# First attention: the odd key tiles split into high and low parts as the even ones are, and the low parts made behind the row maxima

## What is computed

```python
s = (jnp.einsum('bqhd,bkhd->bhqk', qn_b, k_nope, preferred_element_type=jnp.float32)
     + jnp.einsum('bqhr,bkr->bhqk', qr_b, k_rope, preferred_element_type=jnp.float32))
p = jax.nn.softmax(s * scale, axis=-1).astype(v.dtype)
return jnp.einsum('bhqk,bkhd->bqhd', p, v)
```

## Time and profile before

| | |
|---|---|
| median of three runs | 3052.82 us |
| the profiled execution | 3052.03 us |
| its span from first to last instruction | 3050.3 us |
| granted TensorE clock, mean of the span | 0.991 of full speed |
| TensorE (matmul) busy | 2938.4 us, 96% |
| VectorE busy | 1974.5 us, 65% |
| ScalarE busy | 1462.9 us, 48% |

### The profile page before, as it was taken

How to read it: one execution, slowest core, us unless ns; L and a number is a source line. 1 busy time by engine, 2 the same in 40 slices (tenths; PEclk the granted TensorE clock), 3 DMA queues, 4 the chain that set the end, 5 groups by cost and what they waited for, 6 DMA issues and landing times. The chain is left out here.

```text
span 3050.3 us, 46806 instructions
## 1 busy us (share of the span) xinstructions
PE 2938.4 (96%) x18638; PEld 2340.8 (77%) x18638; DVE 1974.5 (65%) x3424; ACT 1462.9 (48%) x2678; POOL 0.2 (0%) x4
## 2 busy tenths in 40 slices
PE   8999999999999999999999989889899999999998
PEld 4676666688888888888888878777778887778886
DVE  4755766658666657877555476777655676656775
ACT  5324555645333334564334377566533555454443
POOL 0000000000000000000000000000000000000000
PEclk9999999999999999999999999999999999999999
DMA  7530000052333347553333342000054334456654
GB/s 277 198 127 1 1 1 1 15 166 73 90 104 104 104 136 272 179 176 104 111 111 110 124 131 58 30 24 24 3 171 167 125 104 145 148 189 241 239 187 148
DMA packets 257018, 359.75 MB, mean 118 GB/s; under 512 B 12832, under 2 KB 142496, under 8 KB 253600
## 3 DMA queue, kind: packets, MB, share of 16 engines
q1 hardware_dynamic: 256800, 356.76, 35.2%
HBM read 272.29 MB, written 84.41 MB: 117 GB/s over the span
## 5 line engine op out<-in xcount | busy, mean ns | idle before, releaser
L206 PE MATMUL ps<-ffn_h,wh 128*128 128x512 f32 x2176 | 671.7, 390 | 6.3 <-DVE ob L1372 5.4
L443 DVE TENSOR_TENSOR wl<-wr,wh 128x512 fp32r<-128x512 f32 x610 | 402.3, 686 | 300.0 <-ACT wh L419 297.6
L419 ACT ACTIVATE wh<-wr 128x512 fp32r<-128x512 f32 x610 | 360.4, 624 | 454.7 <-PE ps L206 345.1
L206 PEld LDWEIGHTS ps<-ffn_h,wh 128*128 128x128 f32 x2176 | 407.4, 188 | 95.3 <-DVE ob L1372 9.6
L206 PE MATMUL ps<-ffn_h,wl 128*128 128x512 f32 x1088 | 423.4, 389 | 0.0
L206 PE MATMUL ps<-in_h,wh 128*128 128x512 f32 x1200 | 369.9, 389 | 2.1 <-DVE ob L1372 2.1
L206 PE MATMUL ps<-wh,wh 128*128 128x512 f32 x756 | 294.8, 390 | 3.3 <-DVE wl L443 3.1
L206 PE MATMUL ps<-wh,wl 128*128 128x512 f32 x756 | 294.2, 389 | 0.0
L206 PE MATMUL ps<-wl,wh 128*128 128x512 f32 x756 | 294.1, 389 | 0.0
L206 PEld LDWEIGHTS ps<-in_h,wh 128*128 128x128 f32 x1200 | 225.0, 188 | 49.4 <-DVE ob L1372 2.5
L206 PEld LDWEIGHTS ps<-ffn_h,wl 128*128 128x128 f32 x1088 | 204.3, 188 | 42.5
(11 more groups left out here) (407 smaller groups left out, 5258.0 us busy)
## 6 DMA issues: line engine op xcount, KB each, us to landing
hid<-ob SPq DMA_DIRECT2D x174, 256.0 KB, 2.3
wr<-hid SPq DMA_DIRECT2D x84, 512.0 KB, 4.8
wr<-in_w_down SPq DMA_DIRECT2D x72, 512.0 KB, 4.3
wr<-in_w_up SPq DMA_DIRECT2D x54, 512.0 KB, 4.4
wr<-in_w_in SPq DMA_DIRECT2D x42, 512.0 KB, 4.8
kept<-ob SPq DMA_DIRECT2D x84, 256.0 KB, 2.0
late<-in_w_ada SPq DMA_DIRECT2D x16, 1024.0 KB, 5.9
wr<-in_w_out SPq DMA_DIRECT2D x32, 512.0 KB, 4.4
```

Source lines behind the costliest of these rows:

```text
L206: return e.op.matmul(out, left, right, start=start, stop=stop, skip_group_check=True)
L419: e.op.activation(self.rows(s)[0], src, ACT.Copy).then_inc(*e.event(self.name + "_act", ("w_high", self.name, s)))
L443: e.op.tensor_tensor(lo, src, hi.bitcast(F32), ALU.subtract).then_inc(*e.event(self.name + "_dve", ("w_low", self.name, s), *done))
```

## The change

1. Odd key tiles are split too: `exponential` makes `Ph` for every step, `low` makes `Pl` for every step, `value` is an `mm3` for every step. The values of the odd key tiles get a high and a low part `VOh`, `VOl` instead of `V1`; their side job gains one subtraction.
2. In `step_vector` the low part of step n + 1 moves from the front of the step to behind the side job and the maxima, for all n.
3. The split exponentials get four pairs of tiles, three of which lie in the first 12 KB, where `X` lies; `VOl` lies there as well. So the loads of `x` move to the queue of the output projection, and wait until the last `value` is done.

```diff
@@ __init__, parts
-        self.V1 = [k.sb("V1", [128, 5, 128], 34.5 + 32 * i) for i in range(2)]
+        self.VO = [pair("VO", [128, 5, 128], (34.5 + 32 * i, 16 + 2.5 * i)) for i in range(2)]
-        self.P = [pair("P", [128, 512], at) for at in ((178, 180), (37, 53), (128, 130))]
+        self.P = [pair("P", [128, 512], at) for at in ((178, 180), (0, 2), (4, 6), (8, 10))]
...
-        i = n // 2 % 2
-        return self.P[2 if i and n >= self.STEPS - 20 else i]
+        return self.P[n % 4]
@@ value
-        if n % 2 == 0:
-            e.wait_ge(("p_low", n))
-            x = mm3(e, o, [x[:, kt // 2, :] for x in self.V[h % 2]], [x[:, :] for x in self.parts(n)], kt == 0, False)
-        else:
-            e.wait_ge(("exp", n))
-            x = mm(e, o, self.V1[h % 2][:, kt // 2, :], self.E[n % 4][:, :], False, kt == 9)
+        e.wait_ge(("p_low", n))
+        V = (self.V, self.VO)[n % 2][h % 2]
+        x = mm3(e, o, [x[:, kt // 2, :] for x in V], [x[:, :] for x in self.parts(n)], kt == 0, kt == 9)
@@ exponential
-        e.wait_ge(("score", n), (("value" if n % 2 else "p_low"), n - 4) if n >= 4 else None)
+        e.wait_ge(("score", n), ("p_low", n - 4) if n >= 4 else None)
         e.op.activation(x, self.bank(n % 3), ACT.Exp).then_inc(*e.event("att_exp", ("exp", n)))
-        if n % 2 == 0:
-            e.wait_ge(("exp", n), ("value", n - 4) if n >= 4 else None)
-            e.op.activation(self.parts(n)[0][:, :], x, ACT.Copy).then_inc(*e.event("att_high", ("p_high", n)))
+        e.wait_ge(("exp", n), ("value", n - 4) if n >= 4 else None)
+        e.op.activation(self.parts(n)[0][:, :], x, ACT.Copy).then_inc(*e.event("att_high", ("p_high", n)))
@@ side_vector, values
-            e.wait_ge(("v_high", h, i), ("v_whole", h, i))
+            e.wait_ge(("v_high", h, i), ("v_odd_high", h, i))
             e.op.tensor_tensor(lo, self.v_side(i, 0), hi.bitcast(F32), ALU.subtract).then_inc(*e.event("att_dve", ("v_low", h, i)))
+            hi, lo = [self.v_place(x, h, i) for x in self.VO[h % 2]]
+            e.op.tensor_tensor(lo, self.v_side(i, 1), hi.bitcast(F32), ALU.subtract).then_inc(*e.event("att_dve", ("v_odd_low", h, i)))
@@ step_vector
-        if 0 <= n + 1 < self.STEPS and n % 2:
-            self.low(e, n + 1)
         if n > self.BEGIN and self.side_job(n - 1):
             self.side_vector(e, *self.side_job(n - 1))
...
         for m in self.maxima(n) if n < self.STEPS else []:
             self.max_vector(e, m)
+        if 0 <= n + 1 < self.STEPS:
+            self.low(e, n + 1)
@@ FirstOut.sync (the four loads of x leave FirstAttention.sync)
+        self.rows.sync(e, self.x_again)
+
+    def x_again(self, e):
+
+        v = self.k.d["x"].rearrange("(t p) n -> p t n", p=128)
+        e.wait_ge(("value", self.att.STEPS - 1))
+        for tp in range(4):
+            e.op.dma_start(self.k.X[:, 2 * tp:2 * tp + 2, :], v[:, 2 * tp:2 * tp + 2, :]).then_inc(*e.load(f"x{tp}", ("x_for_out1", tp)))
```

More of the change, by code:

```diff
@@ L2292, in side_read @@
         what, h, i = self.side_jobs[j]
-        return {"q": [("q_psum", h, i), ("q_cos", h, i)], "row": [("row_high", h, i)]}.get(what, [(what + "_low", h, i)])
+        return {"q": [("q_psum", h, i), ("q_cos", h, i)], "row": [("row_high", h, i)], "v": [("v_odd_low", h, i)]}.get(what, [(what + "_low", h, i)])
     def sync(self, e):
@@ L2301, in sync @@
         e.op.dma_start(self.wq[:, :, :], d["w_q"].rearrange("(k p) n -> p k n", p=128)).then_inc(*e.load("w_q", "w_q"))
-        v = d["x"].rearrange("(t p) n -> p t n", p=128)
-        for tp in range(4):
-            e.op.dma_start(self.k.X[:, 2 * tp:2 * tp + 2, :], v[:, 2 * tp:2 * tp + 2, :]).then_inc(*e.load(f"x{tp}", ("x_for_out1", tp)))
     def queries(self, h, i):
@@ L2361, in value @@
         if kt == 0:
-            e.wait_ge(("v_ones", h % 2), *[(w, h, i) for w in ("v_low", "v_whole") for i in range(2)], ("unit_read", u - 2) if u >= 2 else None)
-        if n % 2 == 0:
-            e.wait_ge(("p_low", n))
-            x = mm3(e, o, [x[:, kt // 2, :] for x in self.V[h % 2]], [x[:, :] for x in self.parts(n)], kt == 0, False)
-        else:
-            e.wait_ge(("exp", n))
-            x = mm(e, o, self.V1[h % 2][:, kt // 2, :], self.E[n % 4][:, :], False, kt == 9)
+            e.wait_ge(("v_ones", h % 2), *[(w, h, i) for w in ("v_low", "v_odd_low") for i in range(2)], ("unit_read", u - 2) if u >= 2 else None)
+        e.wait_ge(("p_low", n))
+        V = (self.V, self.VO)[n % 2][h % 2]
+        x = mm3(e, o, [x[:, kt // 2, :] for x in V], [x[:, :] for x in self.parts(n)], kt == 0, kt == 9)
         x.then_inc(*e.event("att_value", ("value", n)))
@@ L2455, in side_scalar @@
             e.op.activation(self.v_place(self.V[h % 2][0], h, i), self.v_side(i, 0), ACT.Copy).then_inc(*e.event("att_act", ("v_high", h, i)))
-            e.op.activation(self.v_place(self.V1[h % 2], h, i), self.v_side(i, 1), ACT.Copy).then_inc(*e.event("att_act", ("v_whole", h, i)))
+            e.op.activation(self.v_place(self.VO[h % 2][0], h, i), self.v_side(i, 1), ACT.Copy).then_inc(*e.event("att_act", ("v_odd_high", h, i)))
         else:
@@ L2488, in ones @@
         e.op.tensor_scalar(self.V[i][1][:, :, ones], one, 0.0, None, ALU.mult).then_inc(*e.event("att_dve", ("v_zero", i)))
-        e.op.tensor_copy(self.V1[i][:, :, ones], one).then_inc(*e.event("att_dve", ("v_ones", i)))
+        e.op.tensor_scalar(self.VO[i][1][:, :, ones], one, 0.0, None, ALU.mult).then_inc(*e.event("att_dve", ("v_odd_zero", i)))
+        e.op.tensor_copy(self.VO[i][0][:, :, ones], one).then_inc(*e.event("att_dve", ("v_ones", i)))
     def row(self):
@@ L2651, in sync @@
     def sync(self, e):
-        self.rows.sync(e)
+        self.rows.sync(e, self.x_again)
[4 more added lines that the diff above has]
+            e.op.dma_start(self.k.X[:, 2 * tp:2 * tp + 2, :], v[:, 2 * tp:2 * tp + 2, :]).then_inc(*e.load(f"x{tp}", ("x_for_out1", tp)))
 class Feed:
```

## The result

The changed kernel takes 3068.61 us (median of four runs, 3064.42 to 3072.58) against 3052.85 us of the kernel before: ratio 1.0050, 95% interval 1.0033 to 1.0068. It is slower by 15.8 us, where 6.8 were forecast; 3068.6 lies just outside the range. The direction and the first mechanism were right, the size was not.

The account below looks back on a forecast made before the run. The prediction took TensorE to bound the kernel, attention included. Its terms, 0.5 + 3 x 0.9 + 3 x 1.2 + 0 = +6.8 us, on an expected 3052.8 gave 3059.6 us, range 3051 to 3068.

Parts of the forecast that it names:

- The query jobs: Places 4 and 6, heads 0 to 6: stand of 1.03 us at the first (net +0.85), net +0.12 at the second.
- The start of head 0: Head 0: one more fill of a constant ahead of its first low part costs 0.26 us more; head +0.5.
- The value jobs: Places 8 to 11: splitting odd values adds VectorE work, low parts stand behind it; net +0.13 us.
- the walk: Going through the attention's steps with the timeline's distances: 14.2 us saved, 21 us waited, sum +6.8 us.
- The other steps: Places 1 and 3: savings kept, -0.33 us; places 11 to 19: savings less waits of 0.12 once in three steps, -0.5.
- Heads 1, 3, 5: Reciprocals at places 11 to 18 make VectorE the bound: +0.1 in place of -0.5 there, +0.9 us per head.
- Heads 2, 4, 6: Quotient and catl at places 9 and 10 cost about 0.6 us more, place 0 costs 0.3; +1.2 per head.
- Head 7: No maxima, ScalarE falls behind slowly; 1.8 us saved, 1.8 waited, last product ends where it did: 0.
- A: Rival: the saving wins, only the query job's stand at place 4 shows; 7.0 us faster, 3046; 6%.
- B: Rival: about even; head 0 and each other head +0.3, head 7 -1.5; +0.6 us, 3053.5; 38%.
- C: Rival: VectorE is the bound at its unpacked durations, ScalarE likewise; +6.8 + 9 us, 3068; 10%.
- D: Rival: the loads of x come too late or hold the output weights up; +5 to +10 us, 3067; 2%.

Follow-up runs that it names:

- e2: Kernel before with one edit: low parts, still of even steps alone, stand behind side jobs and maxima; 3059.0 us, ratio 1.0023.
- second execution: The changed kernel profiled once more with no edit; its four runs gave 3068.62 us, ratio 1.0060, and its attention took 371.5 us.
- e4: Changed kernel, but in the product of values the fp32r product that reads the low part comes third, behind its own wait; 3052.79 us, ratio 1.0003.
- e9: Changed kernel without 21 of the 24 pieces of reciprocals at places 11 to 18 of heads 1, 3 and 5; one execution, 3068.47 us.
- e3: Changed kernel with the low part of every step at the front again, ahead of side job and maxima; 3054.45 us, ratio 1.0006.
- e8: Kernel before with only the four loads of x moved behind the attention, in the output projection's queue; 3050.7 us, ratio 1.0000.
- e1: The changed kernel once more, no edit; 3068.62 us (3067.42 to 3072.11), ratio 1.0060.

## Why the prediction was right in kind and wrong in size

| | forecast | measured |
|---|---|---|
| head 0 | +0.5 | +1.4 |
| heads 1, 3, 5, each | +0.9 | +2.0 |
| heads 2, 4, 6, each | +1.2 | +2.3 |
| head 7 and its last product | 0 | +0.4 and +0.5 |
| loads of x | 0 | 0 |
| sum | +6.8 | +15.3 |

- **The query jobs.** Right: the stand is 1.02 us against 1.03. Both jobs together were 1.15 in stretch 8 to 11 (1.03 + 0.12); measured 1.36, and in e2 the same. The 0.2 missing are the size of two restarts, and both products (the second stands 0.49) are followed by one.
- **The start of head 0.** Right: its first product of values stands 1.68 us by the starts, 1.42 before, so 0.26 more as forecast.
- **The value jobs.** Right: from the product of step 8 to that of step 11, head 0 of the second execution loses 0.16 against before; the walk had 0.13.
- **The failed step is "The other steps".** It kept the savings at places 1 and 3 (-0.33) and gave -0.5 for places 11 to 19, with a wait of 0.12 once in three steps. Stretch 0 to 4 is 0.35 longer in heads 1, 3 and 5 instead, because of the stand of 0.56 and the restart at place 19, which the walk didn't look at: two maxima and their minimum stand ahead of that low part. Stretch 11 to 20 is 0.07 longer in head 0 instead of shorter. In head 0 the stands of this stretch are small, as walked: 0.14, 0.09 and 0.16 us by the starts in the second execution. But each has a restart behind it, and e4 shows what the lateness costs: with 0.46 us more time for each low part the same order takes 18.26 in heads 1, 3 and 5 and 17.74 in head 0, less than before the change.
- **The term that was left out of every step** is the restart. In the second execution 58 of 160 triples begin with 0.28 to 0.34 between their first two products where 0.23 or 0.24 is the rule, against 3 of 80 before: 5.7 us more, two thirds of the 8.5 that are missing. By the distances between starts TensorE stands 25.3 us ahead of products of values, against 3.5 before. These 21.8 us are near the 21 that the walk had waited, though partly at other places; the restarts come on top. All this is read from the timelines; no experiment took a restart away without its wait. One was to be seen before the change: the product at 593.54, which had waited, has its second at 593.88.
- **Heads 1, 3, 5.** VectorE is busy in 96% of places 11 to 20 there, as forecast. The extra over a head without reciprocals was forecast at 0.6 (0.1 in place of -0.5), and e9 gives 0.6. Right in size, in part by luck: the low part takes 0.60 between starts and not 0.54, and VectorE isn't the whole bound, since e4 does the same work in 0.86 us less.
- **Heads 2, 4, 6.** Forecast 0.3 more than heads 1, 3, 5, measured 0.3 more: 0.27 at places 0 to 4 and 0.1 at 11 to 20, less 0.05 at 4 to 8.
- **Head 7.** "The last product ends where it did" was wrong by 0.9: both last products wait for their low part, 0.64 and 0.34 us by the starts, and each restarts.
- **The rivals.** A and B are excluded by the result, C (VectorE and ScalarE unpacked) would give this time but not for this reason: e3 has the same load and is 16.9 us shorter in the attention. ScalarE's exponential and copy are 1.15 us apart in head 7, as taken; only VectorE's low part lies between C's two values, at 0.60. D was excluded by e8.
- **The line to no change.** The chances had slower at 0.53, which was too near to even: the terms that the walk left out, the restarts and the stand at place 19, all add time.

## What to carry to other kernels

When work is moved off the bounding engine and its result comes back just in time, count the stands one by one, the short ones too, and add the restart to each; here 46 stands of 0.1 to 0.6 us, 15 us in all and 5 more for their restarts, took more than the 14.2 us that were saved. Where several products read a split operand, let those that read the part that is ready first go first, and wait for the late part only before the last: it took back 15 us here without moving any work, which made this kernel as fast as before the change and no faster. And ask at each place of a loop what now stands ahead of the moved instruction, instead of choosing one place for all steps.

## What the runs showed that was not expected

- A triple of fp32r products of 512 columns that waited for a semaphore has 0.34 us between its first two starts, one that didn't 0.23 to 0.24.
- TensorE's clock fell to its lower level (0.50 of full speed) at 247 us behind stands of 0.7 and 1.5 us in one execution, and stayed full behind the same stands in the profiled execution of e1: 1.5 us in head 0.
- The order edit alone, with not one instruction more or less, cost 8.3 us in the attention.
- In the last head ScalarE, not TensorE, is full once every tile has its copy (9.76 of 10.0 us from 605 to 615), and splitting the odd tiles won nothing there.
